# A gate tile held over into the last stage, its branch operands turned one group to a chunk, and two branches in another order

## What is computed

```python
proj = rms_norm(x) @ w_in                      # 16592 columns
o_a = gdn_branch(...)                          # gated delta rule, 1024 columns
o_b = rwkv7_branch(...)                        # RWKV-7, 1024 columns
y   = gelu(s5 scan ...)                        # 1024 columns
o_c = y * sigmoid(y @ glu_w + glu_b) * silu(z)
branches = jnp.stack([o_a, o_b, o_c], axis=2)
branch_proj = jnp.einsum('blnc,ncd->blnd', branches, w_branch)
gates = jax.nn.sigmoid(gate_logits + gate_b)   # 3 x 2048 columns of proj
merged = jnp.sum(gates * branch_proj, axis=2)
x = x + merged @ w_out
out = rms_norm(x, final_norm_w)
```

## Time and profile before

| | us |
|---|---|
| median of 3 runs | 2337.25 |
| lowest and highest | 2332.89, 2341.16 |
| span of the profiled execution | 2345.3 |
| PE busy in it | 2200.1 (94%) |
| DVE, ACT busy | 1557.9 (66%), 1070.7 (46%) |

### The profile page before, as it was taken

The page is one execution under the profiler, slowest core; times in us unless marked ns, Lnnn a source line. Parts: engine busy times, 40 slices in busy tenths (PEclk is TensorE's granted clock), DMA queues, the critical chain, the costliest instruction groups (busy, mean ns, idle before and its releaser), DMA issues.

```text
span 2345.3 us, 35225 instructions
## 1 busy us (share of the span) xinstructions
PE 2200.1 (94%) x14268; PEld 1816.3 (77%) x14268; DVE 1557.9 (66%) x2302; ACT 1070.7 (46%) x1488; POOL 115.8 (5%) x188
## 2 busy tenths in 40 slices
PE   7999889999999999999999889997899999989997
PEld 6889668887888888887777777775687777767886
DVE  5665575557995555658999776665945556567754
ACT  5444565445444655554343653333544223245443
POOL 0000001001001001000000100010010000011000
PEclk9999999999999999999999999999999999999999
DMA  7666337666878448766665634358684433377753
GB/s 237 188 193 198 116 115 258 238 227 224 274 278 309 149 146 285 275 208 240 227 224 179 243 106 156 127 197 312 216 313 153 144 114 122 125 285 246 251 186 121
DMA packets 222482, 481.15 MB, mean 205 GB/s; under 512 B 14896, under 2 KB 51552, under 8 KB 217584
## 3 DMA queue, kind: packets, MB, share of 16 engines
q1 hardware_dynamic: 200112, 372.91, 47.8%
q0 software_dynamic: 22208, 105.99, 12.2%
HBM read 421.45 MB, written 57.40 MB: 204 GB/s over the span
## 4 chain that ended last, share of the span: by engine, by line
PE 63%; DVE 22%; DMA 6%; ACT 4%; issue 4%; POOL 0%; ACTq 0%; SPq 0%; DVEq 0%; POOLq 0%
PE mm_acc L294 36%; PE mm_acc L299 18%; DVE mm_lo L211 6%; DMA mm_raw<-in_w_in 2%; ACT mm_hi L204 1%; DVE s_q L2942 1%; DVE s_p L2927 1%; DVE s_r L2935 1%; DVE s_p L2928 1%; DVE s_r L2937 1%; DMA rwk_src<-rw_rh 1%; DVE gdn_cv L1844 1%; PE in_turn L381 1%; DMA in_xt<-proj 1%; DMA tail_gb<-in_s_glu_b 1%
## 5 line engine op out<-in xcount | busy, mean ns | idle before, releaser
L211 DVE TENSOR_TENSOR mm_lo<-mm_raw,mm_hi 128x1024 fp32r<-128x1024 f32 (+4 forms) x672 | 791.1, 1185 | 511.9 <-ACT mm_hi L204 502.9
L204 ACT CAST mm_hi<-mm_raw 128x1024 fp32r<-128x1024 f32 (+4 forms) x672 | 682.1, 1019 | 811.5 <-PE mm_acc L299 778.5
L294 PE MATMUL mm_acc<-mm_hi,mm_aT_hi 128*128 128x512 f32 (+5 forms) x2208 | 873.3, 396 | 19.3 <-ACT mm_hi L204 14.4
L294 PE MATMUL mm_acc<-mm_hi,mm_aT_lo 128*128 128x512 f32 (+5 forms) x2208 | 852.5, 387 | 0.0
L299 PE MATMUL mm_acc<-mm_lo,mm_aT_hi 128*128 128x512 f32 (+5 forms) x2208 | 579.8, 385 | 13.2 <-DVE mm_lo L211 12.8
L294 PEld LDWEIGHTS mm_acc<-mm_hi,mm_aT_hi 128*128 128x128 f32 x2208 | 422.4, 191 | 103.0 <-ACT mm_hi L204 15.3
L299 PEld LDWEIGHTS mm_acc<-mm_lo,mm_aT_hi 128*128 128x128 f32 x2208 | 414.2, 190 | 93.8 <-DVE mm_lo L211 21.2
L294 PEld LDWEIGHTS mm_acc<-mm_hi,mm_aT_lo 128*128 128x128 f32 x2208 | 422.5, 191 | 69.7 <-issue 1.0
L256 ACT ACTIVATE mm_stage<-mm_acc,mm_row_scale 128x512 f32<-128x512 f32 (+3 forms) x104 | 64.5, 672 | 82.9 <-PE mm_acc L299 82.8
L294 PE MATMUL mm_acc<-mm_hi,in_yT_hi 128*128 128x512 f32 x256 | 100.9, 394 | 0.2 <-ACT mm_hi L204 0.2
L294 PE MATMUL mm_acc<-mm_hi,in_yT_lo 128*128 128x512 f32 x256 | 99.7, 389 | 0.0
(11 more groups left out here) (634 smaller groups left out, 2071.2 us busy)
## 6 DMA issues: line engine op xcount, KB each, us to landing
mm_raw<-in_w_in SPq DMA_DIRECT2D x384, 512.0 KB, 4.8
mm_raw<-in_w_out SPq DMA_DIRECT2D x96, 512.0 KB, 5.3
mm_raw<-in_w_in SPq DMA_DIRECT2D x72, 464.0 KB, 4.0
mm_raw<-in_w_branch SPq DMA_DIRECT2D x48, 512.0 KB, 5.5
proj<-mm_stage SPq DMA_DIRECT2D x46, 512.0 KB, 3.0
mm_raw<-in_w_in SPq DMA_DIRECT2D x32, 416.0 KB, 4.6
home_tab<-s5t_tab POOLq DMA_DIRECT2D x4, 2048.0 KB, 9.3
s_tab<-home_tab POOLq DMA_DIRECT2D x8, 1024.0 KB, 5.9
```

The source lines that it names most:

```text
L204: self.nc.scalar.copy(self.hi[:, c % RING, :, 0:t.w], self.raw[:, c % RAW, :, 0:t.w]).then_inc(self.hi_done, 1)
L211: self.nc.vector.tensor_tensor(self.lo[:, c % RING, :, 0:t.w], self.raw[:, c % RAW, :, 0:t.w], self.hi[:, c % RING, :, 0:t.w].bitcast(F32) ...
L294: nc.tensor.matmul(self.acc[s][m][:, 0:t.w], t.aT[a][:, k, m * P:(m + 1) * P], self.hi[:, c % RING, k - k0, 0:t.w], start=(k == 0 and a == ...
```

## The change

One gate tile, the last of `late`, is no longer multiplied in the RWKV stage (`late[5:-1]`) but as the first tile of the last stage (`held`). The calls of the last stage are re-ordered: each of the 12 operand jobs is followed by one chunk (`turn_among` on PE, `copies_among` on ACT and DVE), and the branches go 0, 1, 2 instead of 0, 2, 1. `late` is also split so that a tile of `(N_IN - O_SZ) % TN` columns would come first.

```diff
-    ORDER = (0, 2, 1)
...
-        plan = [jobs_a, jobs_c, jobs_b] + jobs_m
+        plan = [jobs_a, jobs_b, jobs_c] + jobs_m
...
-                mm.sp(sp, 2 * n_glu + len(order) * n_br + n_last)
+                mm.sp(sp, n_held + 2 * n_glu + len(order) * n_br + n_last)
...
+                    if i == len(order) - 1:
+                        mm.wait_stored(pool, held)
                     gates(i)
...
+                def turn_among(i):
+                    for job in plan[i]:
+                        turner.turn(pe, [job])
+                        mm.pe(pe, 1)
+                    turned(i)
+
                 ph.enter(pe)
+                mm.pe(pe, 2)
+                pe.wait_ge(y_in, 16)
+                row_turner.turn(pe, jobs_r[0:2])
+                mm.pe(pe, n_held - 6)
+                turn_among(0)
                 for i in range(2):
                     pe.wait_ge(y_lo, i + 1)
                     mm.pe(pe, 2)
-                pe.wait_ge(y_in, 16)
-                row_turner.turn(pe, jobs_r[0:2])
-                turn(0)
-                mm.pe(pe, 2)
                 row_turner.turn(pe, jobs_r[2:4])
-                mm.pe(pe, 2 * n_glu - 6)
-                turned(0)
-                mm.pe(pe, n_br)
-                turn(1)
-                turn(2)
-                turned(1)
-                mm.pe(pe, n_br)
-                turned(2)
+                mm.pe(pe, 2 * n_glu - 4)
+                turn_among(1)
+                turn_among(2)
                 mm.pe(pe, n_br)
...
+                def copies_among(i):
+                    for j, job in enumerate(plan[i]):
+                        turner.copy_hi(act, [job], base[i] + j)
+                        mm.act(act, 1)
+
                 ph.enter(act)
...
-                mm.act(act, 2)
+                mm.act(act, n_held - 4)
+                copies_among(0)
                 act.wait_ge(z_in, 32)
                 nc.scalar.activation(z[:, :, :], z[:, :, :], ACT.Silu).then_inc(silu, 1)
-                mm.act(act, n_glu - 2)
-                copies(0)
                 sigmoid(0)
-                mm.act(act, n_glu + n_br)
-                copies(1)
-                copies(2)
-                mm.act(act, 2 * n_br)
+                mm.act(act, 2 * n_glu)
+                copies_among(1)
+                copies_among(2)
+                mm.act(act, n_br)
...
-                mm.dve(dve, n_glu)
+                mm.dve(dve, n_held - 4)
+                copies_among(0)
                 dve.wait_ge(silu, 1)
...
                 gate_rows(0)
-                copies(0)
                 gate(0)
-                mm.dve(dve, 2)
+                mm.dve(dve, 4)
                 gate_rows(1)
-                mm.dve(dve, n_glu)
-                dve.wait_ge(sig, 2)
-                zrows = z[:, :, :].rearrange("p m (h c) -> p h m c", h=2)
-                TT(zrows, zrows, yrows, ALU.mult).then_inc(oc_done, 1)
-                gate(1)
-                mm.dve(dve, n_br - 2)
-                copies(1)
-                copies(2)
-                product(1)
+                mm.dve(dve, 2 * n_glu - 4)
+
+                def combine():
+                    dve.wait_ge(sig, 2)
+                    zrows = z[:, :, :].rearrange("p m (h c) -> p h m c", h=2)
+                    TT(zrows, zrows, yrows, ALU.mult).then_inc(oc_done, 1)
+                    gate(1)
+
+                copies_among(1, combine)
+                copies_among(2, lambda: between(1))
                 product(2)
...
-            for_s5, for_gdn, for_rwkv, late = (mm.add(p2["w_in"], home, c) for home, c in (
-                (None, (O_SU, O_SZ)), (proj, (0, c_rwkv)), (proj, (c_rwkv, O_SU)), (proj, (O_SZ, N_IN))))
+            narrow = (N_IN - O_SZ) % TN
+            for_s5, for_gdn, for_rwkv, narrow, late = (mm.add(p2["w_in"], home, c) for home, c in (
+                (None, (O_SU, O_SZ)), (proj, (0, c_rwkv)), (proj, (c_rwkv, O_SU)), (proj, (O_SZ, O_SZ + narrow)), (proj, (O_SZ + narrow, N_IN))))
+            late = narrow + late
...
-                    rwkv(nc, "rwk", a, mm, for_gdn + for_rwkv, late[5:], proj, *rw, carry, rp["lnx_w"], rp["lnx_b"], ob, rows.load)
-                    tail(nc, "tail", mm, rows, glu, branch, out2, proj, oa, ob, p2["s5_glu_b"], p2["gate_b"], x3, a["final_norm_w_2"], out[0])
+                    rwkv(nc, "rwk", a, mm, for_gdn + for_rwkv, late[5:-1], proj, *rw, carry, rp["lnx_w"], rp["lnx_b"], ob, rows.load)
+                    tail(nc, "tail", mm, rows, late[-1:], glu, branch, out2, proj, oa, ob, p2["s5_glu_b"], p2["gate_b"], x3, a["final_norm_w_2"], out[0])
```

More of the change, by code:

```diff
@@ L2959, in load, with tail @@
         pool.dma_start(self.yt[:, :, :], self.yg.rearrange("(k p) t -> p k t", p=P)).then_inc(self.y_in, 16)
-def tail(nc, name, mm, early, glu, branch, last, proj, oa, ob, glu_b, gate_b, x, norm, out):
+def tail(nc, name, mm, early, held, glu, branch, last, proj, oa, ob, glu_b, gate_b, x, norm, out):
     K, NBR = S_W, 3
     KT, TILES = K // P, D // TN
-    ORDER = (0, 2, 1)
     SLOTS = 3
@@ L3011, in tail @@
         for n in range(TILES):
-            for i, b in enumerate(ORDER):
-                branch[n * NBR + i].aT = bT[b]
+            for b in range(NBR):
+                branch[n * NBR + b].aT = bT[b]
         for t in last:
             t.rows, t.rows_in = xt, (res_in, 16)
-        n_glu, n_br, n_last = ticks(glu[:1]), ticks(branch[:1]), ticks(last)
+        n_held, n_glu, n_br, n_last = ticks(held), ticks(glu[:1]), ticks(branch[:1]), ticks(last)
         order = [(n, i) for n in range(TILES) for i in range(NBR)]
@@ L3036, in gates @@
                     n, j = order[i]
-                    c0 = ORDER[j] * D + n * TN
+                    c0 = j * D + n * TN
                     pool.dma_start(gt[:, i % SLOTS, :, :], rowsv(proj)[:, :, O_GL + c0:O_GL + c0 + TN]).then_inc(gate_in[i % SLOTS], 16)
-                    pool.dma_start(gbt[:, i % SLOTS, :], bcast_rows(gate_b[ORDER[j], n * TN:(n + 1) * TN])).then_inc(gate_in[i % SLOTS], 16)
+                    pool.dma_start(gbt[:, i % SLOTS, :], bcast_rows(gate_b[j, n * TN:(n + 1) * TN])).then_inc(gate_in[i % SLOTS], 16)
                 pool.dma_start(ab[:, :, :], rowsv(oa)).then_inc(a_in, 16)
@@ L3173, in _, with copies_among @@
                 copies = lambda i: turner.copy_lo(dve, plan[i], base[i])
+                def copies_among(i, after=lambda: None):
+                    for j, job in enumerate(plan[i]):
+                        turner.copy_lo(dve, [job], base[i] + j)
+                        mm.dve(dve, 1)
+                        if j == 1:
+                            after()
                 def glu_out(t):
@@ L3188, in branch_out @@
                     if j == 0:
-                        dve.wait_ge(turner.turned, base[n + 2] if n >= 2 else base[3])
+                        dve.wait_ge(turner.turned, base[n + 2] if n >= 2 else base[2])
                     if j and 2 * n + j > 1:
@@ L3313, in program @@
             c_rwkv = -(-O_RF // TN) * TN
-            for_s5, for_gdn, for_rwkv, late = (mm.add(p2["w_in"], home, c) for home, c in (
-                (None, (O_SU, O_SZ)), (proj, (0, c_rwkv)), (proj, (c_rwkv, O_SU)), (proj, (O_SZ, N_IN))))
+            narrow = (N_IN - O_SZ) % TN
+            for_s5, for_gdn, for_rwkv, narrow, late = (mm.add(p2["w_in"], home, c) for home, c in (
+                (None, (O_SU, O_SZ)), (proj, (0, c_rwkv)), (proj, (c_rwkv, O_SU)), (proj, (O_SZ, O_SZ + narrow)), (proj, (O_SZ + narrow, N_IN))))
+            late = narrow + late
             glu = mm.add(p2["s5_glu_w"], None)
-            branch = [t for n in range(D // TN) for b in (0, 2, 1) for t in mm.add(p2["w_branch"][b], None, (n * TN, (n + 1) * TN))]
+            branch = [t for n in range(D // TN) for b in range(3) for t in mm.add(p2["w_branch"][b], None, (n * TN, (n + 1) * TN))]
             out2 = mm.add(p2["w_out"], None)
```

## The result

| | median of its runs, us | range, runs |
|---|---|---|
| before | 2338.76 | 2331.09 to 2343.76, 16 |
| changed | 2345.45 | 2338.72 to 2353.26, 16 |

Ratio changed to before **1.0033, interval 1.0022 to 1.0043**: slower by 0.33%, about 7.7 us, where 2.5 us faster was forecast (the two medians, each over all its runs, differ by 6.7 us). That is just beyond the bound of 0.3%, which lies inside the interval, and the median is above the range of 2325.5 to 2343.

What follows compares the result with a forecast made beforehand. PE was taken to set the pace at 2.72 us a chunk. 6.1 us more lost in the RWKV stage and 8.6 less in the last gave -2.5 on 2337.25, so 2334.7 us, range 2325.5 to 2343.

Steps and rivals of the forecast that it cites:

- (a): Gate into the last stage: PE waits 3.0 us there, then pays 1.7 us for the clock.
- (b): Last stage, jobs of branch 0, each covered by a chunk: `hi` and a copy fit on ACT, no loss.
- (c): Last stage, Silu, Sigmoid and held-tile scaling in one ACT row, 10.8 us: PE waits about 2.6, clock takes 1.7.
- (d): Last stage, 8 jobs of branches 1 and 2 over 8 chunks: DVE's 12.2 us fits in 12.6, no loss.
- (e): RWKV stage, one chunk removed ahead of `rwk_src`, one ahead of its second half: 2.72 and 0.9 us more waiting.
- (f): RWKV stage, five chunks removed within the four groups: new waits of 0.1, 2.7, 1.4, 0.2 and -1.9 us.
- Rival 1: Gain comes in full: RWKV's 1.7 us issue stall and slow chunk go, no last-stage clock fall; 2327 us, chance 0.28.
- the harmless wait: PE's clock: a 1.5 us wait costs nothing extra, a long one 1.7 to 2.7; bound between 1.5 and 1.7.
- Rival 2: Slower: thinner cover in the RWKV stage brings three new clock falls, 8.1 us; up to 2344.7 us, chance 0.13.

Runs made afterwards that it cites:

- e5: Changed kernel with the first Sigmoid moved behind two more chunk calls on ACT; ratio to before 1.0044.
- e3_placed: Changed kernel, same 64 RWKV chunks at hand-chosen points, only three in the first ten steps of an inversion; ratio to before 1.0000.
- e6_alternate: Changed kernel, 64 RWKV chunks at chosen points, one to every second inversion step, none before a group's last step; ratio to before 0.9990.
- e8_last_wait: As e6_alternate, but each group's chunk at point 13 moved to 14, ahead of the last inversion step; ratio to before 0.9947.
- e2_hold_only: Kernel before with only the last tile held (64 RWKV chunks), the last stage's other work in its old order; ratio to before 1.0031.
- e1: Kernel before, all 72 RWKV chunks kept, with only the new branch order and the last 8 jobs spread one to a chunk; ratio 0.9989.
- e4: Changed kernel with a second tile held (56 RWKV chunks, 16 held); ratio to before 1.0103.
- e9: On top of e1, all 72 RWKV chunks at chosen points, with chunks at 13 and 14 of each group; ratio to before 0.9937.

## Why the prediction was wrong, step by step

**What bounds the kernel, and what a chunk costs: right.** PE sets the pace, and a chunk moved is 2.72 us moved; the runs are in order by what PE waits and how its clock stands.

**The last stage: right.** (a) 3.0 us at the gate were forecast, 2.06 came, with a slow chunk of 4.57 us behind it (1.7 forecast, 1.7 came). (b) No loss among the jobs of branch 0: right. (c) 2.6 forecast, 2.61 came, again with the 1.7; ACT's row of 10.8 us was forecast term by term and took 10.6 (2079.29 to 2089.9). (d) No loss forecast, 0.92 came, ahead of the first job that turns `tail_z`. Together 10.0 instead of 9.0: the gate was a microsecond cheaper, (d) a microsecond dearer, and 1.1 us are spread over the stretch in no wait. The wait in (c) was also where the Trainium skill (ScalarE: Activation LUTs, "What ACT_TABLE_LOAD costs") would have had 1.4 us more for a drain. The trace disagrees: the first load starts at 2080.84, 0.02 us after the end of the cast before it, and Silu 0.02 us after the load. The 1.42 us before Sigmoid are no drain either, since DVE's sum ended at 2086.75; in e5 the same load ended at 2077.19 and Sigmoid began at 2077.21.

**The RWKV stage: the step that failed.** (e) The waits for `rwk_src` were to grow by 3.6 us and grew by 3.5, but in two parts of 1.7 and 1.9 where 2.7 and 0.9 had been put; that the sum came out is partly luck. The 0.76 us at `rwk_be` was not seen. (f) was to cost 2.5 in all and costs 5.1. New waits of PE by groups of heads, in us:

| group | forecast | came |
|---|---|---|
| first | 0.1 | 0.9 |
| second | 4.1 | 2.3 |
| third | 0.2 | 2.6 |
| last | -1.9 | -0.8 |

In the last, 0.6 is a wait of a chunk for DVE at 2042.34.

The sentence that fell is "Where a chunk goes between steps of the inversion, the steps follow each other with almost no wait (...), and PE gets its 2.72 back in full". I had read from the absence of waits in the trace of before that there was nothing to cover. It was the chunks that covered it: without them the steps wait for DVE (L1457 1.03 to 2.2 us, L1448 0 to 1.1) and for instructions (2.2 to 3.1 us), 3.3 us that I had at 0.3. Of the rest, the products of the second group were forecast at 2.7 and took 1.8, its state 1.4 and took 1.5, and the last group's `rwk_QT` went to 2.41 as forecast. A cover that works leaves no row; I had to ask for each chunk taken away what the steps behind it would wait for, from the lengths of the DVE operations between them. e3_placed, e6_alternate and e8_last_wait show this from the other side: with the number of chunks kept, a chunk moved by a point or two inside the inversions bares or covers 1 to 2 us a group.

Rival 1 took the stall of 1.7 us before as belonging to one place of the instruction stream. That one did go (1871.3), but two others came, 1.42 us at 1798.87 and 1.71 at 1942.08.

**The clock: wrong bound, and more scatter than I allowed.** I put the harmless wait at up to 1.5 us. The wait of 1.46 us for the state, in the second group of the changed kernel:

```profile
1899.20 0.69 PE L2404 MATMUL rwk_bank<-rwk_Hs,rwk_alT 128*128 128x128 f32 x2 [1.46 <-DVEq L2524]
...
1901.68 0.77 PE L294 MATMUL mm_acc<-mm_hi,mm_aT_hi 128*128 128x512 f32 x1
1902.25 0.63 PE L294 MATMUL mm_acc<-mm_hi,mm_aT_lo 128*128 128x512 f32 x1
```

and in the last group of the kernel before:

```profile
2039.78 0.49 PE L2404 MATMUL rwk_bank<-rwk_Hs,rwk_alT 128*128 128x128 f32 x2 [1.46 <-DVEq L2524]
...
2041.14 0.48 PE L294 MATMUL mm_acc<-mm_hi,mm_aT_hi 128*128 128x512 f32 x1
2041.46 0.39 PE L294 MATMUL mm_acc<-mm_hi,mm_aT_lo 128*128 128x512 f32 x1
```

0.63 us against 0.39 for a matmul, 1.2 GHz against 2.4 (a granted clock of 0.50 and of 1.00). The place does not explain it: e2_hold_only has the wait where the changed kernel has it, with the same code in the stage, and its next chunk takes 3.01 us instead of 5.09. In the seven such waits of all executions at even points the clock fell in three (changed, e1, e5) and not in four (before, e2, twice in e4). There is no single length that parts the two. The Trainium skill (TensorE: Matmul & The Clock Gate, Part 1) has the chip look at PE's activity in a window that runs freely, so that the number of slow matmuls varies from run to run; by that a wait's price depends on when it comes, and these traces fit it, though none shows the window.

How much the clock adds is not to be read from the profiled executions, which are single ones (that of before has a mean clock of 0.978, that of e2 0.981). What the long chunks of the stage have above 3.0 us adds up to 13.6 and 12.9 us in the two with 72 chunks at even points, and to 18.2, 12.2 and 13.0 in the three with 64, on average 1.2 us more. But the mean granted clock is on record for every run, and over the changed kernel's 16 runs it is 0.9789, over the 60 runs of before that have it, those of the experiments (three chips, 0.9810, 0.9812 and 0.9809), 0.9810. Time at half speed lowers the mean clock by half its share; if all of it is PE's work, it also costs half its share, and 0.0021 less costs 2340 x 0.0021 = 4.9 us; among the runs of either kernel on one chip the time rises by 0.9 to 1.7 us for each 0.001, which gives 2 to 3.5. So I estimate that the clock adds 2 to 5 us over the whole execution. Rival 2 had it as three more falls, 8.1 us, for which I gave 0.13: its mechanism is there, at a quarter to some half of its size. That its number (2344.7) came out within a microsecond is luck, since it held none of the new waits in the inversions.

**The sum.** Forecast -2.5. The new waits are 3.3 us more than forecast (9.4 for 6.1) and the last stage loses 1.0 more: +1.8, and the clock of the RWKV stage, whose change had been put at nothing, comes on top. Taken as a whole, PE's waits grow by 9.4 us in the RWKV stage and shrink from 12.2 to 5.6 in the last, +2.8; with the 2 to 5 for the clock that is +5 to +8. Measured are +6.7 by the medians and +7.7 by the ratio. How the clock's part divides among the stages stays open, since with the same code S differs by up to 8 us between profiled executions. That the new order is not what costs is shown by e2_hold_only, which has the same ratio without it.

**The parts that cost nothing.** The order of the branches and the 208-column tile: e2_hold_only has neither, and the same ratio as the changed kernel, so together with the spread turns they bring nothing while the tile is held.

## What to carry to other kernels

Filler work that is dealt evenly hides waits without leaving a row. Before taking some of it away, work out for each place what its neighbours would wait for, and before moving filler to another stage, try where it stands in its own: here the points were worth 0.5 to 0.9%, and the tile that was moved cost 0.3%.
A wait costs its length and often again half of it or more in a slow clock, but the second part varies from run to run; judge such a change by medians and by waits added up, not by one profiled span.
Take a chunk away from dense tiny matmuls with care as well: they can run out of instructions with all their data there.

## What the runs showed of the hardware that I had not expected

- PE stops for up to 3.15 us amid 32x32 matmuls with no semaphore in between (e3_placed), and for 3.46 us at a chunk right behind them (e8_last_wait): 13.0 us in one stage of e3_placed, 2.2 in the kernel before, 3.2 in e9. With a chunk to every second step of 64 it is less in all (5.9 us in e6, 6.9 in e8), but not gone. 36 of 42 such stalls end 1.24 to 1.59 us after a transfer of the instruction queue.
- The granted clock fell after three waits of 1.46 us and not after four others, in one case at the same place of the same code.
- Loads of 512 KB took 11.7 us from issue to landing beside a 2 MB load in e5, and a wait that PE's row puts down to ACT was a DMA's. In the changed kernel the same loads took 8.3 us (median of six) and ACT waited 3.57 us for one; whether moving Sigmoid made them later is not shown.
